# Scores of a sample's last two quads of keys issued behind the values of the sample ahead

## What is computed

```python
def dilated_attn_sample(q, k_new, v_new, k_buf, v_buf, dil, slopes):
    ...
    j = jnp.arange(A_STEPS + 1)                       # 129 keys for each query
    idx = buf + jnp.arange(t)[:, None] - dil * j[None, :]
    ...
    scores = jnp.einsum('bthd,btjhd->bhtj', q, kg) * (dh ** -0.5)
    scores = scores - slopes[:, None, None] * (dil * j)[None, None, :]
    m = jnp.max(scores, axis=-1, keepdims=True)
    p = jnp.exp(scores - m)
    den = jnp.sum(p, axis=-1)
    o = jnp.einsum('bhtj,btjhd->bthd', p, vg) / ...den
    lse = m + jnp.log(den)
```

## Time and profile before

| | us |
|---|---|
| median of 3 runs | 1317.78 |
| lowest and highest | 1312.26, 1319.25 |
| the profiled execution, whole | 1314.65 |
| its span in the trace | 1313.0 |
| mean granted TensorE clock in it | 0.982 of full |
| PE busy in the span | 1237.6 (94%) |
| DVE, ACT, POOL busy | 661.7, 548.7, 194.0 |
| the rounds of the samples, first key transpose to the projection `ga0` | 639.2 to 791.6 |

### The profile page before, as it was taken

One profiled execution on the slowest core, in us unless ns is written; L12 is line 12 of the kernel. 1 busy time (PEld: TensorE's weight loads), 2 busy tenths in 40 slices (PEclk: granted clock), 3 DMA queues, 4 the chain that ended last, 5 costly groups with the idle time before them and its releaser, 6 DMA issues.

```text
span 1313.0 us, 17979 instructions
## 1 busy us (share of the span) xinstructions
PE 1237.6 (94%) x7160; PEld 941.9 (72%) x7160; DVE 661.7 (50%) x920; ACT 548.7 (42%) x878; POOL 194.0 (15%) x228
## 2 busy tenths in 40 slices
PE   4899999999999999999889999999989999999996
PEld 1677877776778887887756666747757887777762
DVE  1328513222161205032377551255687888888877
ACT  3623313002272126214433332211446787777852
POOL 1202200020000010001200010100034122222320
PEclk9899999999999999999799999999989999999999
DMA  9552221154443454537689995911399999999982
GB/s 357 209 209 76 94 64 64 65 190 173 152 146 85 159 178 176 171 128 275 238 295 382 384 374 172 304 64 53 104 318 296 371 374 374 372 373 378 366 301 91
DMA packets 126235, 293.96 MB, mean 224 GB/s; under 512 B 10160, under 2 KB 10288, under 8 KB 121496
## 3 DMA queue, kind: packets, MB, share of 16 engines
q1 hardware_dynamic: 108216, 243.57, 52.7%
q0 software_dynamic: 17952, 49.44, 10.5%
HBM read 269.91 MB, written 30.42 MB: 229 GB/s over the span
## 4 chain that ended last, share of the span: by engine, by line
PE 78%; DMA 11%; DVE 4%; ACT 4%; issue 2%; POOL 2%; SPq 0%; DVEq 0%; ACTq 0%; POOLq 0%
PE psum L997 18%; PE psum L999 17%; PE psum L998 17%; PE psum L985 5%; PE psum L1039 5%; DMA arena<-in_cache_kv_w_dram 3%; DMA arena<-in_w_gate_dram 2%; PE psum L1360 2%; PE psum L1196 2%; PE psum L1012 2%; DMA arena<-in_w_ada_dram 2%; PE psum L1268 2%; ACT arena L1564 1%; POOL slots_d L915 1%; PE psum L1174 1%
## 5 line engine op out<-in xcount | busy, mean ns | idle before, releaser
L997 PE MATMUL psum<-part,part 128*128 128x512 f32 (+1 forms) x1088 | 442.4, 407 | 10.6 <-DVE part L1942 5.0
L999 PE MATMUL psum<-part,part 128*128 128x512 f32 (+1 forms) x1088 | 429.4, 395 | 0.0
L998 PE MATMUL psum<-part,part 128*128 128x512 f32 (+1 forms) x1088 | 429.3, 395 | 0.0
L997 PEld LDWEIGHTS psum<-part,part 128*128 128x128 f32 (+1 forms) x1088 | 227.4, 209 | 74.3 <-issue 24.8
L999 PEld LDWEIGHTS psum<-part,part 128*128 128x128 f32 (+1 forms) x1088 | 227.3, 209 | 40.1
L998 PEld LDWEIGHTS psum<-part,part 128*128 128x128 f32 (+1 forms) x1088 | 228.1, 210 | 35.7
L2360 DVE TENSOR_TENSOR part<-arena,part 128x2048 fp32r<-128x2048 f32 x96 | 218.9, 2291 | 33.5 <-ACT part L1792 32.3
L1891 DVE TENSOR_TENSOR part<-arena,part 128x2048 fp32r<-128x2048 f32 x42 | 96.4, 2301 | 254.5 <-PE psum L1039 228.7
L1792 ACT ACTIVATE part<-arena 128x2048 fp32r<-128x2048 f32 x94 | 179.7, 1919 | 45.1 <-DMA arena<-in_w_down_dram 19.5
L1564 ACT ACTIVATE arena<-psum 128x512 f32<-128x512 f32 (+3 forms) x140 | 75.9, 567 | 248.4 <-PE psum L999 202.7
L1575 ACT ACTIVATE part<-arena 128x2048 fp32r<-128x2048 f32 x42 | 80.0, 1910 | 173.2 <-DMA arena<-in_w_in_dram 168.6
(11 more groups left out here) (289 smaller groups left out, 1071.2 us busy)
## 6 DMA issues: line engine op xcount, KB each, us to landing
arena<-in_w_in_dram SPq DMA_DIRECT2D x34, 1024.0 KB, 5.5
arena<-in_cache_kv_w_dram SPq DMA_DIRECT2D x16, 2048.0 KB, 11.9
arena<-in_w_gate_dram SPq DMA_DIRECT2D x32, 1024.0 KB, 9.9
arena<-in_w_up_dram SPq DMA_DIRECT2D x32, 1024.0 KB, 9.4
arena<-in_w_down_dram SPq DMA_DIRECT2D x32, 1024.0 KB, 10.2
arena<-in_w_ada_dram SPq DMA_DIRECT2D x24, 1024.0 KB, 7.7
arena<-in_cache_kv_w_dram SPq DMA_DIRECT2D x16, 1024.0 KB, 9.0
arena<-in_w_ada_final_dram SPq DMA_DIRECT2D x8, 1024.0 KB, 7.9
```

The costliest lines, as they stand in the source:

```text
L997: nc.tensor.matmul(out_, hi, w_hi, start=start, stop=False)
L998: nc.tensor.matmul(out_, hi, w_lo, start=False, stop=False)
L999: last_product[0] = nc.tensor.matmul(out_, lo, w_hi, start=False, stop=stop)
```

## The change

Quads 2 and 3 of sample `b` are no longer issued inside `scores(b)`. PE issues them behind `attend(b - 1)`: in `scores`, tiles 7 to 12 now follow each other with only the exponentials' transposes between them, then come `gather_heads(b - 2)`, `attend(b - 1)`, quad 2, quad 3, and, in rounds 1 to 4, the prompt's tile. The bank `ss{b}` is therefore given out behind `so{b - 1}`. On DVE the masking of `so{b - 1}` is moved with it: it stood behind sample `b`'s weights and now stands ahead of sample `b`'s bias. ACT's list stays as it is, and no instruction is added or removed.

```diff
@@ for b in range(NB + 2): (the rings' order) @@
                     tp.stage(f"kt{b}x{x}", 1, KT_USER[x])
-                mm.stage(f"ss{b}", 1, "dve")
...
             if 1 <= b <= NB:
                 mm.stage(f"so{b - 1}", 1, "dve")
+            if b < NB:
+                mm.stage(f"ss{b}", 1, "dve")
...
@@ PE @@
             def scores(b):
-                lead = (3, 7, 11, 13)
+                lead = (3, 7, 13)
                 x = 0
-                for quad in range(4):
+                for quad in range(3):
                     while x < lead[quad]:
                         if b and x == PT_AT:
                             turn_exponentials(b - 1)
                         turn_keys(b, x)
                         x += 1
-                    if quad == 3 and b >= 2:
-                        gather_heads(b - 2)
-                    quad_scores(b, quad)
+                    if quad < 2:
+                        quad_scores(b, quad)
+                if b >= 2:
+                    gather_heads(b - 2)
...
                 if 1 <= b <= NB:
                     attend(b - 1)
+                if b < NB:
+                    quad_scores(b, 2)
+                    quad_scores(b, 3)
@@ DVE @@
+            def own_values(c):
+
+                m = mm.first[f"so{c}"]
+                mm.wait_filled(dve, m)
+                if c:
+                    tp.wait_filled(dve, tp.first[f"ot{c - 1}"])
+                V.tensor_tensor(om, mm.bank(m), c_("dmask"), ALU.mult).then_inc(mm_dve, 1)
...
+                    if b:
+                        own_values(b - 1)
                     dve.wait_ge(sb_in, 16)
                     m = mm.first[f"ss{b}"]
                     mm.wait_filled(dve, m)
...
-                if b >= 1:
-                    c = b - 1
-                    m = mm.first[f"so{c}"]
-                    mm.wait_filled(dve, m)
-                    if c:
-                        tp.wait_filled(dve, tp.first[f"ot{c - 1}"])
-                    V.tensor_tensor(om, mm.bank(m), c_("dmask"), ALU.mult).then_inc(mm_dve, 1)
+                if b == NB:
+                    own_values(NB - 1)
```

## The result

| | before | after |
|---|---|---|
| median of 4 runs, us | 1318.51 | 1340.10 |
| lowest and highest | 1312.26, 1322.23 | 1338.61, 1343.04 |
| the profiled execution | 1314.65 | 1343.04 |
| mean granted TensorE clock in it | 0.982 | 0.970 |

The changed kernel is slower by 21.6 us on the medians, ratio 1.0166, 95% interval 1.0138 to 1.0194. Run a second time, beside new runs of before, it took 1337.93, ratio 1.0139 (1.0117 to 1.0160). The forecast was 1338.

The account below looks back on a forecast made before the run. PE's own work (17.6 us a round) and the loads (17.8 us) were taken as level. Waits of 19.3 less 2.6 us, plus 5.6 for the clock, gave 22.3 on 1314.65, so 1337.0; 1338 was taken, range 1328 to 1350.

Parts of the forecast that it names:

- hand-overs 1 to 2 until 4 to 5: PE stands until ACT empties the prompt's tile, then waits 0.1 for tile 0's copy: 2.3 us each, 9.2 together.
- hand-overs 5 to 6, 6 to 7: With 1.53 us of tiles in three free banks, PE then waits for key copies: 2.5 us each, 5.0 together.
- DVE's lateness, rounds 2 to 4: DVE starts tile 1 late, delaying copies and turned exponentials: PE waits 0.8 us more a round, 2.4 together.
- ahead of `ga0`: Behind sample 7's quad 3, PE waits 2.7 us for ACT's and DVE's split of the projection's weights.
- waits for keys that go: Once rounds exceed 17.8 us, loads have time to spare and PE's 2.6 us of waits for keys vanish.
- brings nothing: In round 0 quad 3's wait for copies goes, without gain, because a DMA sets DVE's late start behind it.
- The clock: PE's clock falls behind four of seven new waits, 1.4 us each, 5.6 us; bounds 0 and 9.8 us.
- the clock staying down longer: Rival: falls at every hand-over, half taking a second stretch at 0.50, 36 us in all: 1341 to 1352; chance 0.16.
- the signs named: Expected profile: waits about 2.2, 2.4, 2.7 us, no key waits, rounds about 20.7 and 19.6 plus 1.4 per fall, 330-350 GB/s.
- the clock would not fall: Rival: the clock bears the new waits, leaving 16.7 us, 18 with one fall: 1331 to 1334; chance 0.14.
- the loads cover the waits: Rival: loads set the round, so PE's waits ending before the next landing cost nothing: 1315 to 1321; chance 0.06.
- Faster: Rival: earlier value slots let loads run ahead and last-copy waits go, 3.5 us gained: 1311 to 1314; chance 0.04.

Follow-up runs that it names:

- longer-softmax pair: Three exponentials of each sample issued twice on ACT: in the changed kernel 1351.88 us, ratio 1.0247; in the kernel before 1319.39 us, ratio 1.0006.
- run with fewer values: Kernel before, with four of a sample's 13 value tiles not loaded from sample 1 on: 1313.11 us, ratio 0.9957.
- quad 2 alone: Kernel before, with quad 2 moved behind tile 12 and quad 3 left ahead of the values: 1315.60 us, ratio 0.9984.

## Why the prediction was right

**The bound.** PE and the loads are level in these rounds: right. The longer-softmax pair shows that the hand-overs of the changed kernel lie on the path, and the run with fewer values that the loads cost before something too, 6.2 us in all, of which the rows of the rounds show 2.3.

**The waits.** Terms and measured values:

| term | predicted | measured |
|---|---|---|
| hand-overs 1 to 2 until 4 to 5 | 4 x 2.3 = 9.2 | 4 x 2.26 = 9.1 |
| hand-overs 5 to 6, 6 to 7 | 2 x 2.5 = 5.0 | 2 x 2.47 = 4.9 |
| DVE's lateness, rounds 2 to 4 | 3 x 0.8 = 2.4 | 3 x 0.63 = 1.9 |
| ahead of `ga0` | 2.7 | 2.62 |
| waits for keys that go | -2.6 | -2.6 |

The four terms came from one uncovered hand-over, that of sample 0, read as the model for all others: ACT free after 2.96 us there, after 2.97 here. In round 0 quad 3's wait went and the first tile of round 1 came 1.8 us earlier (0.75 us of that are the first key tile's, 638.44 against 639.19, ahead of all that was changed), but the hand-over of round 0 grew from 5.12 to 6.36, since DVE waits there for a DMA. Quad 0 of round 1 began at 661.30 against 661.91: no more than that first lead, so "brings nothing" was right. Round 1 won its 0.9 and lost 0.6 to two short waits. From quad 0 of round 1 on the waits come to 15.4 us (16.6 less the 1.24 by which the first hand-over grew) against 16.7 predicted.

DVE's term had the size nearly right and the cause wrong. The forecast had DVE late because it starts behind the softmax. With quad 3 alone behind `attend` DVE starts just as late, and the waits are gone; with quad 2 alone it doesn't, and PE waits 1.3 us for DVE. What brings them is that quad 2, 1.06 us of PE's work, no longer stands ahead of the exponentials.

**The clock.** Direction right, size too small. Predicted four falls at 1.4 us, 5.6. The size of one was right: 1.2 to 1.5 us at the hand-overs. The count was not: of the seven new waits six had a fall behind them, five hand-overs and the one ahead of `ga0`, and there were two more in an `attend`, at 1.7 us each. Up to the first product of `ga0`, where only six of them count, the rest of the difference is 7.4 us. What was off is the count, and its premise that only waits of over 2 us matter.

The page "TensorE: Matmul & The Clock Gate" of the Trainium skill (section "A second HAM failure mode: psum-queue depth-cycling") speaks of short idle moments of a cycling PSUM queue between groups, behind which the clock falls and rises again. The trace agrees in kind for the hand-overs, with five of six at 0.50 and one at 1.00 with the same wait; for the falls in `attend` it doesn't show that an idle moment is the cause (last section). By the page's rule the sum was 26.5, by the falls as counted in the forecast 22.3; the medians gave 21.6.

**The sum.** 22.3 us predicted, 22.2 in the trace at the first product of `ga0`, 21.6 on the medians and 18.3 in the repetition (1337.93 - 1319.66). From quad 0 of round 1 on, which leaves out what lies ahead of the change, the trace has 22.8. That it fits so well is partly luck: two misses of opposite sign, 1.3 us too much for waits and 1.8 too little for the rest, and in that rest 8.6 us of falls and 1 us more in round 1 meet PE's own shorter work, which the forecast didn't have. The profiled execution as a whole gave 28.4: the two falls behind that product, 3.2 us, and 3.1 more outside the rounds were not in the sum. Of the signs named, the waits came as said; the rounds were longer than 20.7 and 19.6 us by 0.9 to 1.1 us with one fall and 2.7 with two, and the data rate was mostly below the 330 to 350 GB/s named (324, 297 and 316 in rounds 2 to 4, 273 to 351 behind them).

**The rivals.** That the clock would not fall is out. For the clock staying down longer the forecast has 36 us without a working: seven falls at 1.4 us and half of them once more make 31.4. That the loads cover the waits is out in the changed kernel, where a longer softmax shows up in full. *Faster* was put at the condition that the first key copy ends by 1.4 us behind the last score. The change as written never met it (ACT's copy began 2.97 us behind the bias); with the copies, the queries' spread and `combine` moved, the first key copy ended 1.1 us behind it where no prompt's tile comes first and 1.7 where one does, PE had no such wait, and the kernel became 0.4% faster than before. So the condition was about right; the rival's reason, that the waits for keys go, was not, since PE waited 5.4 us for keys there against 2.6.

## What to carry to other kernels

When work is moved on an engine with no slack, look at what it stood between: here `attend` was the cover for 3 to 4.5 us of another engine's chain, and its move cost 2.3 to 2.5 us of waits in each round, and most times a fall of the clock, although the work is the same. The move pays only together with the other engines' lists: whatever the next piece of PE's work needs (copies, spread queries, a split of weights) has to stand ahead of the chain that waits for the last piece, all of it and not only the part that the first profile names. Price a hand-over from one in the same trace that already lacks the cover.

## What the runs showed of the hardware

PE's clock fell behind waits of 2.26 and 2.47 us, and not always: the waits that end at 704.41 and 749.47 are both 2.26 us long, at the same place of a round, and only the first was followed by 0.50. Nor is it the length of the wait alone: with the exponentials twice the clock stayed up behind a wait of 3.64 us (802.98). It also fell inside `attend` of round 3 (the window at 718.00), where PE had waited 0.32 and 0.31 us in the 5 us ahead and nothing else; the 24 products took 4.48 us against 2.78. The same happened in `attend(7)` behind one wait of 0.94 us (timeline of PE in after); before has the same wait there, and its products took 2.78 us:

```profile
838.71 1.10 PE L1301 MATMUL psum<-arena 128*128 128x512 f32 x2 [0.94 <-ACT arena L1569]
...
840.79 4.48 PE L1308 MATMUL psum<-arena 128*32 128x512 f32 x24
```

The `attend`s of rounds 2 and 4 had the same short waits ahead and kept full clock. And with quad 3 alone behind `attend`, where these short waits are gone, one `attend` fell all the same, 13 us behind the last wait, with the clock at 1.00 in between (windows 770.00 to 773.40 and 775.00 to 779.00):

```profile
766.20 2.15 PE L1269 MATMUL psum<-arena 128*128 128x136 f32 x8 [2.47 <-ACT arena L169]
...
779.35 4.47 PE L1308 MATMUL psum<-arena 128*32 128x512 f32 x24
```

So the short waits are not what it takes. What sets these `attend`s apart was not isolated. Two products that nothing reads, put into the waits, kept the clock at all six hand-overs and brought 5 to 7 us on the medians. They are a patch: with the waits themselves covered the kernel is 19 us faster still (1332.92 - 1313.98; 17 by the ratios).
